# Compression of the prompt's new keys and values in four column tiles of the PE array

## The reference, cut to what matters

```python
def _nsa_compress(kf, w1, pe, w2):
    n_parts = NSA_CMP_LEN // NSA_CMP_STRIDE           # 32 // 16 = 2
    n_cmp = (tk - NSA_CMP_LEN) // NSA_CMP_STRIDE + 1  # 15 for the prompt
    hid = 0.0
    for m in range(n_parts):
        rows = slice(m * NSA_CMP_STRIDE, (m + 1) * NSA_CMP_STRIDE)
        part = jnp.einsum('bnpgd,pdh->bngh', sub + pe[rows][:, None, :], w1[rows])
        hid = hid + part[:, m:m + n_cmp]
    return jax.nn.gelu(hid) @ w2

k_cmp = _nsa_compress(full[:, :, 0], cmp_w1[0], cmp_pe[0], cmp_w2[0])
v_cmp = _nsa_compress(full[:, :, 1], cmp_w1[1], cmp_pe[1], cmp_w2[1])
```

## Time and profile before

| | |
|---|---|
| median of three runs | 2629.42 us |
| the profiled execution's own time | 2629.91 us |
| its span, first to last instruction | 2628.2 us |
| PE busy | 2535.0 us, 96% of the span |
| DVE, ACT and POOL busy | 1406.1, 1328.2 and 773.9 us |
| mean granted clock of PE | 0.976 |
| compression of the new tokens on PE (line 1721) | 64 records, 2148.7 to 2162.7 us |
| attention rounds | about 2206 to 2352 us |

### The profile page before, as it was taken

How to read it: one execution, slowest core, us unless ns; L and a number is a source line. 1 busy time by engine, 2 the same in 40 slices (tenths; PEclk the granted TensorE clock), 3 DMA queues, 4 the chain that set the end, 5 groups by cost and what they waited for, 6 DMA issues and landing times. The chain is left out here.

```text
span 2628.2 us, 50001 instructions
## 1 busy us (share of the span) xinstructions
PE 2535.0 (96%) x17485; PEld 2470.6 (94%) x17485; DVE 1406.1 (54%) x2211; ACT 1328.2 (51%) x1996; POOL 773.9 (29%) x810
## 2 busy tenths in 40 slices
PE   6999999999999988999999999999999998889998
PEld 6999998999999986999999998999999996669997
DVE  6455455554555466655455456654455446765543
ACT  4565444564466336555365332555465334755642
POOL 2333233332233222333133224333133211113331
PEclk8999999999999998999999999999999998889999
DMA  6234343434343440443444443434444453214442
GB/s 221 89 130 145 146 156 115 159 145 152 142 154 144 144 180 1 148 156 136 152 159 144 149 155 116 158 144 144 146 158 147 150 214 113 64 48 155 149 145 99
DMA packets 66305, 366.24 MB, mean 139 GB/s; under 512 B 9154, under 2 KB 21762, under 8 KB 28290
## 3 DMA queue, kind: packets, MB, share of 16 engines
q1 hardware_dynamic: 64530, 356.58, 37.5%
q0 software_dynamic: 1536, 4.20, 0.5%
q10 hardware_dynamic: 144, 4.19, 0.4%
HBM read 361.98 MB, written 4.92 MB: 140 GB/s over the span
## 5 line engine op out<-in xcount | busy, mean ns | idle before, releaser
L322 PE MATMUL bank<-x_hi,w_hi 128*128 128x320 f32 x3336 | 1036.0, 311 | 0.0
L295 ACT ACTIVATE w_hi<-w_raw 128x1024 fp32r<-128x1024 f32 (+1 forms) x641 | 657.5, 1036 | 746.9 <-PE bank L322 721.6
L322 PE MATMUL bank<-x_lo,w_hi 128*128 128x320 f32 x3336 | 1030.9, 309 | 0.0
L322 PE MATMUL bank<-x_hi,w_lo 128*128 128x320 f32 x3336 | 1030.8, 309 | 0.0
L304 DVE TENSOR_TENSOR w_lo<-w_raw,w_hi 128x1024 fp32r<-128x1024 f32 (+1 forms) x641 | 832.4, 1334 | 260.4 <-ACT w_hi L295 260.4
L322 PEld LDWEIGHTS bank<-x_hi,w_hi 128*128 128x128 f32 x3336 | 626.3, 188 | 2.2 <-issue 0.6
L322 PEld LDWEIGHTS bank<-x_hi,w_lo 128*128 128x128 f32 x3336 | 626.3, 188 | 1.3
L322 PEld LDWEIGHTS bank<-x_lo,w_hi 128*128 128x128 f32 x3336 | 626.2, 188 | 0.0
L322 PE MATMUL bank<-h_hi,w_hi 128*128 128x320 f32 x1664 | 519.5, 312 | 12.9 <-POOL h_lo L925 5.6
L322 PE MATMUL bank<-h_hi,w_lo 128*128 128x320 f32 x1664 | 517.9, 311 | 0.0
L322 PE MATMUL bank<-h_lo,w_hi 128*128 128x320 f32 x1664 | 517.8, 311 | 0.0
(11 more groups left out here) (290 smaller groups left out, 2062.9 us busy)
## 6 DMA issues: line engine op xcount, KB each, us to landing
w_raw<-stream SPq DMA_DIRECT2D x289, 1024.0 KB, 4.8
w_raw<-stream SPq DMA_DIRECT2D x32, 768.0 KB, 4.1
n_sel<-pool_sel SPq DMA_DIRECT2D x64, 128.0 KB, 2.1
w_raw<-cmp_w SPq DMA_DIRECT2D x4, 1024.0 KB, 9.4
pages<-pool_cmp SPq DMA_DIRECT2D x32, 128.0 KB, 5.8
pages<-pool_cmp POOLq DMA_DIRECT2D x32, 128.0 KB, 5.2
w_new<-cmp_w ACTq DMA_DIRECT2D x1, 4096.0 KB, 15.4
const<-const SPq DMA_DIRECT2D x1, 1533.0 KB, 10.6
```

The lines of the kernel that those rows point to most:

```text
L295: act.activation(w_hi[:, (2 * n + half) % HALVES, 0:k, :], raw[:, n % RAW, 0:k, P * half:P * half + P], ACT.Copy).then_inc(hi_ready, 2 if ...
L322: mm = pe.matmul(acc, w[:, s, kk, :], a[:, k0 + kk, :], start=(first and kk == 0 and w is w_hi and a is act_hi), stop=(last and kk == k - ...
```

## The change

The 32 positions of a window are cut into two halves of 8 pair positions. Keys and values, first and second half, make four sums; each has a block of 32 output partitions of its own in bank 7 (31 used), and the four are taken in turn at each of eight steps. The number of matmul calls stays 32. ACT copies the four blocks one by one, each into its own partitions of `n_hrow`, which is now 128 x 256 and is set to zero first, since partitions 31, 63, 95 and 127 are not written by the copies. The turning is no longer a transpose but a matmul over all 128 partitions with `n_fold` (128 x 31, one for keys and one for values), which has a one where the column's row in the first half is and a one where it is in the second: it turns and adds the two halves at once. DVE makes `n_fold` by adding two slices of the identity and clears `n_hrow`, both at the head of `pair_up`.

```diff
-            n_hrow = w1_space("n_hrow", [HROWS, 2, 256])
+            n_hrow = w1_space("n_hrow", [P, 256])
+            n_fold = w1_space("n_fold", [P, 2, 32])
             def hidden():
                 pe.wait_ge(w1_landed, 16)
-                pe.wait_ge(pairs_ready, 4)
+                pe.wait_ge(pairs_ready, 6)
                 pe.wait_ge(std_ready, st["norm"] + 1)
+                for i in range(8):
+                    for kv in range(2):
+                        for half in range(2):
+                            pp, at = 8 * half + i, 32 * (2 * kv + half)
+                            pairs = n_pairs[:, kv, :, :].rearrange("p g n -> p (g n)")[:, pp:pp + N_STRIDE * (HROWS - 1) + 1:N_STRIDE]
+                            mm = pe.matmul(bank[7][at:at + HROWS, 0:256], pairs, w1_new[:, kv, pp, :], start=(i == 0), stop=(i == 7))
+                mm.then_inc(nhid_ready, 1)
+            def turn_hidden():
+                pe.wait_ge(nhid_copied, 4)
                 for kv in range(2):
-                    for pp in range(16):
-                        pairs = n_pairs[:, kv, :, :].rearrange("p g n -> p (g n)")[:, pp:pp + N_STRIDE * (HROWS - 1) + 1:N_STRIDE]
-                        mm = pe.matmul(hid_bank[kv][0:HROWS, 0:256], pairs, w1_new[:, kv, pp, :], start=(pp == 0), stop=(pp == 15))
-                    mm.then_inc(nhid_ready, 1)
-            def turn_hidden():
-                for kv in range(2):
-                    pe.wait_ge(nhid_copied, kv + 1)
                     for ht in range(2):
-                        tr = pe.transpose(hid_bank[kv][:, 256 + 32 * ht:256 + 32 * ht + HROWS], n_hrow[:, kv, P * ht:P * ht + P],
-                                          cst("ident")[0:HROWS, 0:HROWS])
+                        tr = pe.matmul(hid_bank[kv][:, 256 + 32 * ht:256 + 32 * ht + HROWS], n_hrow[:, P * ht:P * ht + P],
+                                       n_fold[:, kv, 0:HROWS], start=True, stop=True)
                     tr.then_inc(nhid_turned, 1)
+        def flat_half(fold, h):
+            return fold[:, :, h:h + 1, :].rearrange("p k h c -> p k (h c)")
 # act_nsa
-            for kv in range(2):
-                act.wait_ge(nhid_ready, kv + 1)
-                act.activation(n_hrow[:, kv, :], hid_bank[kv][0:HROWS, 0:256], ACT.Copy).then_inc(nhid_copied, 1)
+            act.wait_ge(pairs_ready, 6)
+            act.wait_ge(nhid_ready, 1)
+            for at in range(0, P, 32):
+                act.activation(n_hrow[at:at + HROWS, :], bank[7][at:at + HROWS, 0:256], ACT.Copy).then_inc(nhid_copied, 1)
 # dve_nsa, pair_up
+                dve.memset(n_hrow[:, :], 0.0).then_inc(pairs_ready, 1)
+                fold = cst("ident").rearrange("p (k h c) -> p k h c", k=2, h=2)
+                dve.tensor_tensor(n_fold[:, :, :], flat_half(fold, 0), flat_half(fold, 1), ALU.add).then_inc(pairs_ready, 1)
                 dve.wait_ge(evacuated, st["g0"] + 2)
```

## The result

The changed kernel takes 2624.53 us (median of 12 runs, 2622.3 to 2628.82), the kernel before 2633.2 in the same comparison (12 runs, 2629.35 to 2637.27): ratio 0.997, 95% interval 0.9961 to 0.9978. That is faster by 0.30% where 0.37% was forecast, with the bound of 0.3% inside the interval; 2624.53 lies 4.7 us above the forecast of 2619.8 and just outside its range of 2617.0 to 2624.5.

What follows compares the result with a forecast made beforehand. The prediction took PE, busy 96% of the span, to bound the kernel. Its terms, -10.34 for `hidden` and +0.45 for the turning, summed to -9.9 us, giving a forecast of 2619.8 us (-0.37%), range 2617.0 to 2624.5.

Steps and rivals of the forecast that it cites:

- What bounds the kernel: At the compression PE is busy throughout, so a microsecond taken from PE there is a microsecond off the end.
- The matmuls of `hidden`, -10.34: Compression's 64 records on PE: four blocks side by side take 3.31 us instead of 13.65, saving 10.34 us.
- The turning, +0.45: Between chunks 4 and 5 on PE: eight records with 128 stationary columns take 0.9 us, +0.45 us over before.
- ACT, DVE, weight stream at 0: ACT's four copies, DVE's clearing and addition, and the transfers for chunks 6 and 7 are ready before needed; cost 0.
- So it moves whole: Tail after chunk 7, loads and attention rounds shift with PE; the clock below 1.00 there is allowed +-1.5 us.
- The base: Starting time of the sum: profiled execution 2629.91 us, median of three runs 2629.42 us.
- (1): Compression's matmuls: only neighbouring records on different blocks overlap, 7.3 us instead of 13.96, kernel 2623.5 us; chance 12%.
- (2): Compression's matmuls: the tiles don't overlap, gain 0, turning +0.45, kernel 2630.0 us; chance 8%.
- (3): Compression's matmuls: each block change waits for the record before, 24.3 us against 13.65, kernel 2640.5 us; chance 3%.
- wrong if the attention rounds lengthen: Stated sign of failure: the attention should begin some 10 us earlier and last as long as before.

Runs made afterwards that it cites:

- before_turn: Kernel before with the hidden layer's four transposes replaced by the same four calls as plain matmuls; 2637.49 us, ratio 1.0024 to the kernel before.
- order_one: Changed kernel with only the order of the 32 calls turned, one output block finished before the next; 2633.5 us, ratio 1.0006 to the kernel before.
- cut: Kernel before with only the first 4 of 16 pair positions of the compression computed; 2623.8 us, ratio 0.9974 to the kernel before.
- the padded one: Changed kernel with 48 unused float32 matmul calls directly behind the compression, run twice; 2637.56 and 2636.12 us, ratios 1.0028 and 1.002 to the kernel before.
- before_extra: Kernel before with only the change's additions on DVE and ACT, none on PE; 2635.18 us, ratio 1.0015 to the kernel before.
- order_two: Changed kernel with keys and values as the outer loop, so two blocks take turns at a time; 2622.57 us, ratio 0.9964 to the kernel before.
- order_pairs: Changed kernel with two calls on the same block before the next block follows; 2626.19 us, a single execution.
- before_nudge: Kernel before with two float32 matmuls of ones by the identity ahead of the last two transposes; 2634.03 us, ratio 1.001 to the kernel before.

## Why the prediction was right, and where it failed

- **What bounds the kernel.** Right. PE was on the path throughout the stage: the chunk behind, the turning and the first scores moved by the sum of the terms.
- **The matmuls of `hidden`, -10.34.** Right: 3.31 us from first start to last, as worked out from two-block rows; four records run side by side. The factor of 2.38 for three column tiles, from the Trainium skill, page "TensorE: Matmul & The Clock Gate", Part 3, section "Measured speedup vs the span model", scaled to four as an estimate, would have been 1 us off here: the trace has 13.65/3.31 = 4.1.
- **The turning, +0.45.** 0.96 - 0.60 = +0.36; size off by 0.09. Taking the row with 128 stationary columns and not scaling down for 31 moving ones was right: eight records in 0.97 us.
- **ACT, DVE, weight stream at 0.** Right, by the rows above. The covers were there, and the splits of chunks 6 and 7 are released by PE.
- **"So it moves whole", ±1.5 us.** This is the step that failed. Up to the first scores it moved whole, 10.04 us. The forecast said that the attention would last as long as before. The attention and the output projection then took 7.4 us more in the first two profiles, with PE busy at 1.2 GHz for 20 us more; by the means the loss is 3.1 ± 0.4. The forecast had seen the granted clock of 0.84 in the earlier trace rows and took a shift against it to be as likely good as bad, within 1.5 us. Of nine altered kernels without fillers in the gaps none gained more than its stage did, and before_turn, order_one, cut, the padded one and before_extra lost 3 to 6 us each beside the changed one (order_two, -7.1 ± 1.5 of -7.4, order_pairs with its single execution, and before_nudge are undecided). So the allowance was too small, and in these kernels the loss lay on the slow side. Nothing in the one profile that the forecast had could tell that.
- **The base.** The sum stood on a profiled execution of 2629.91 and a median of three of 2629.42. The mean of 121 executions is 2632.05, with more than two fifths of them above 2631.5. Against that base, the forecast of -9.9 would have said 2622.1, and the loss of 3.1 makes it 2625.3, the mean of the 36 (the 3.1 was taken from these means, so this is bookkeeping and no test). The rivals' totals start from bases that differ by a few tenths of a microsecond (2640.5 stands on the median, 2623.5 on 2629.7); nothing hangs on it.
- **Rivals.** (1), (2) and (3) are refuted by the 3.31 us and by order_pairs, (1) although its time, 2623.5, is the nearest to what was measured. The nearness is chance: a right number for a wrong reason. What the forecast named under "wrong if the attention rounds lengthen" is what happened.

**What stays open.** That PE's lower clock takes part in the loss is shown by the start of the output projection and by the fillers. That it is the whole of it is not: two executions of the kernel before with about as much of it differ by 5.6 us, and the profiles show that it falls in other places. Why it falls better in the kernel before than in its variants stays open. Start time, plain turning, overlap and the extra DVE and ACT work were each taken alone, and each lost or was undecided without explaining the others. Whether some exact phase between the rounds and the weight stream matters, or whether the kernel before is simply one favourable draw of many, would need many more variants than were run.

## What to carry to other kernels

Float32 matmuls with at most 32 output partitions (here 31, with 256 moving columns) can be dealt out over four blocks of 32 output partitions at the full factor, if at most two calls of one block stand in a row; no other form was run. Before a saving in one stage is booked at the end, look at the granted clock of the stages behind it: where PE has gaps and the clock is below 1.00, compare length, busy time and clock of the same stretch in several executions of both kernels, and not the mean clock alone, and try fillers in the gaps first; here they were worth 8.8 us, nearly as much as the change's stage. And where a few microseconds decide, don't take three runs for the base.

## What was not expected of the hardware

- Records of different column blocks start out of program order (order_one: 2149.999 with three earlier records still waiting), two of them 6 to 7 ns apart in the changed kernel; by the starts a block seems to hold four records.
- Two executions of one program differ by 5.6 us in one stretch (181.9 and 187.5 us) at almost the same mean granted clock (0.88 and 0.89): 14 us more at 1.2 GHz in the six rounds cost nothing, 10 us more in the last round and the output projection went with 4.5 us.
- Useless matmuls shorten a stretch: 120 records more, 9.3 us less (189.27 to 180.02), at a granted clock of 0.97 instead of 0.83.
- A change that adds only work to DVE and ACT beside a busy PE (before_extra) costs 3.8 ± 1.1 us elsewhere.
